# A two-block transformer layer on one core: how the chosen tokens are counted in the router, and which semaphores a few loads share

## The chip, the cores and the metric

The kernel runs on one core of a Trainium2 chip, written engine by engine: each engine has a program of its own, and they meet at semaphores. The metric is the device time of one execution in microseconds, the median of the runs. All data are float32.

## The reference, cut to what matters

Two blocks run one after the other on 256 tokens of width 1024. The first has a modulation, a Fourier and convolution mixer, and then an expert-choice layer of 16 experts. The second has two kinds of attention, a gate and a final norm. The change touches the router of the experts and some waits of the second block.

```python
logits = h @ w_router + b_router          # 256 tokens x 16 experts
probs = softmax(logits)
vals, idx = top_k(probs.T, 32)            # each expert takes 32 tokens
xe = h[idx]                               # 16 x 32 x 1024
y = (silu(xe @ w_gate_e) * (xe @ w_up_e)) @ w_down_e
x = x + gate_f * scatter_add(y * vals, idx)
x = rms_norm(x, g_final)                  # then the second block:
u = rms_norm(x, mix_norm_g) @ w_in_2      # q, k, v of both attentions, z
s = q @ k.T * scale + bias                # bias: slopes times distance, masks
```

The experts' weights are 16 x 3 x 8 MB, and each is read once.

## The kernel before

**Weights.** SyncE (SP) issues all large loads into a ring of 16 places of 1 MB in SBUF and a few more beside it (`ring`, `extra`, `late`). It waits until PE has released a place (`slot_used`), and then loads the next piece. `load_expert` (L601) loads the experts' pieces. For each expert PE computes the hidden products (`hidden_product`, L1142, 8 k-steps for gate and 8 for up, a place released after each), then the product with `w_down_e` (L1169), and scatters the rows into PSUM (L1180). The first expert's weights, and some of the second's, fit into the ring before routing is finished; after that SP has to wait for PE's first release.

**Router.** It runs once, between the mixer's last product and the first expert, on PE, DVE and ACT in turn. The order is: last quarters of `x` (L1994, L1995), turned by PE (`turn_x`, L1018) and kept (L2000); partial logits (`logit_parts`, L1026) copied by DVE (L2015); sums of the parts (L1068), `logit` (L2021), softmax, `prob` turned to expert rows (L1073). On those 16 rows of 256 tokens DVE takes the eight largest and strikes them out, four times (`V.max` L2033, `match_replace` L2034). Then it marks the struck ones (`is_lt`, L2036), sums the marks along the row with a scan (L2037) and multiplies sum and mark (L2038), which numbers each chosen token 1 to 32. PE turns these numbers back to token rows (L1082), DVE copies them (`slot_of`, L2040), builds the selection matrix of the first expert (L2042), PE gathers its rows (`gather`, L1090), DVE copies them, PE turns them (`turn_rows`, L1098), DVE scales and shifts them (L2052, L2054) into `cur[0]`, and the first hidden product starts.

**x's turns into banks.** The experts' results are added up in PSUM banks 4 to 7, which first get `x` itself, turned: 16 products of a 128x128 piece of `x` with the identity (L1077). In PE's program all 16 stand between the turn of `prob` and the turn of the numbers.

**Second block.** Its entry norm's gain `gfin` and the attention bias `bias` are loaded by GpSimd's queue (POOL). `gfin` (L714) is issued during the second expert. `bias` (3 MB, L716) goes to places of the ring that are free only late: POOL waits until PE has used the first weight piece of `q_diff`. They have a semaphore each, `side_loaded` and `bias_loaded`. DVE's program is in a fixed order; the part that matters is

```python
            split("k_diff", 0)
            dve.wait_ge(side_loaded, 16)
            # four products x * gfin into xg (L2252), each waits for a sum of squares
            split("k_diff", 1)
            norm_rows(2, halves=True)
            # further norms (roots by ACT, L1372), then
            split("q_dil", 0)
```

`split` turns a weight piece into a high and a low part: ACT copies the high part (L1380), DVE subtracts (L1763), and PE multiplies three times (L734 to L736, 24 such groups of one row or 5.5 us a piece here) only when the low part is there. `score_rows` (L2132) is the first that reads `bias`; its scores come from PE (L1222).

Of the kernel before, what the change touches and what calls it, by code (L numbers as in the profile page):

```python
# [20 lines left out]
ALU = mybir.AluOpType  # L21
# [3 lines left out]
P = 128  # L25
SEQ, D = 256, 1024
# [84 lines left out]
MIX_BANK = ((0, 2), (1, 3), (4, 5), (6, 7))  # L111
TURN_BANK = ((0, 0), (1, 1), (2, 2), (3, 0))

X_MIXED = 2 * WO


def build(nc, t, out):
    ctx = ExitStack()
    with ctx:
        def sem(name):  # L120
            return ctx.enter_context(nc.semaphore(name))
# [115 lines left out]
        logit_rows = gm_row[:, 256:512]  # L237
        left_t, order_t = gm_row[:, 256:512], squares_out[0]
        p_rows = shaped(gm_row[:, 512:1024], t=TT, c=SEQ)
# [33 lines left out]
        gain_loaded, gain_turned, gain_ready = sem("gain_loaded"), sem("gain_turned"), sem("gain_ready")  # L273
        dft_loaded, side_loaded, bias_loaded = (sem(n) for n in ("dft_loaded", "side_loaded", "bias_loaded"))
        late_loaded, row_bias_loaded = sem("router_and_gate_rows_loaded"), sem("row_bias_loaded")
# [32 lines left out]
        mask_ready, mask_turned = sem("mask_ready"), sem("mask_turned")  # L308
        gathered, rows_kept, rows_turned = sem("gathered"), sem("rows_kept"), sem("rows_turned")
        scaled, cur_ready, gw_turned, gwt_ready = sem("scaled"), sem("cur_ready"), sem("gw_turned"), sem("gwt_ready")  # L310
# [3 lines left out]
        p_loaded, pp_loaded, pp_done, pp_kept = sem("p_loaded"), sem("w_pp_loaded"), sem("pp_done"), sem("pp_kept")  # L314
        row_scale_ready, z_gated = sem("row_scale_ready"), sem("z_gated")
# [358 lines left out]
        def _(pool):  # L674
# [37 lines left out]
            pool.wait_ge(slot_used, HEAD_SLOTS + RING + 4)  # L712
            pool.dma_start(w_pp, rows_of(t["w_ple_proj_2"][0], (0, D), 0, 2)).then_inc(pp_loaded, 16)
            pool.dma_start(gfin, t["g_final"].partition_broadcast(P)).then_inc(side_loaded, 16)  # L714
            pool.wait_ge(slot_used, first_slot["q_diff"] + 1)
            pool.dma_start(bias, t["bias"].rearrange("(t p) h s -> p t h s", p=P)).then_inc(bias_loaded, 16)  # L716


        @block.tensor
        def _(pe):  # L720
# [337 lines left out]
            turn_x(3, (0,))  # L1058
            for i in range(3):
                pe.wait_ge(xt_act, i + 1)  # L1060
                logit_parts(i)
            pe.wait_ge(x_ready, 8)
            turn_x(3, (1,))
            pe.wait_ge(xt_dve, TT)
            logit_parts(3).then_inc(parts_done, 1)
            pe.wait_ge(parts_kept, 1)
            for tt in range(TT):
                last = mm(psum[:, 5, tt * NE:(tt + 1) * NE], logit_rows[:, tt * P:(tt + 1) * P], stack, start=True, stop=True)  # L1068
            last.then_inc(logits_done, 1)

# [31 lines left out]
            pe.wait_ge(slot_ready, 2)  # L1102
            gather(0)
            turn_rows(0, 1)

            def side_step(j):
# [7 lines left out]
                if j in (3, 5):  # L1114
                    n = j // 2 - 1
                    if n == 0:
                        pe.wait_ge(pt_ready, 1)
                        pe.wait_ge(pp_loaded, 16)
                    for tt in range(TT):
                        if n:  # L1120
                            pe.wait_ge(pp_kept, tt + 1)
                        for k in range(2):
                            last = mm(bank(tt), pt[k][:, tt * P:(tt + 1) * P], w_pp[:, k, n * BANK:(n + 1) * BANK], start=(k == 0), stop=(k == 1))
                        last.then_inc(pp_done, 1)

            def expert(i, h, looped=False, side=False):

                def weights(j, **dims):
# [5 lines left out]
                    return shaped(extra_slot(at) if at >= RING else ring[:, at, :], **dims)  # L1134

                def hidden_product(b):
# [9 lines left out]

                pe.wait_ge(cur_ready, 2 * i + (h + 1))
                hidden_product(0)
# [574 lines left out]
        def _(dve):  # L1723
# [294 lines left out]
            dve.wait_ge(logits_done, 1)  # L2018
            dve.wait_ge(base_ready, 1)
            for tt in range(TT):  # L2020
                ins = V.scalar_tensor_tensor(logit[:, tt, :], psum[:, 5, tt * NE:(tt + 1) * NE], stat[:, 1, 3, tt:tt + 1], base, ALU.mult, ALU.add)  # L2021
            link(ins)
# [8 lines left out]
            left = psum[0:NE, 1, 0:SEQ]  # L2031
            for _ in range(CAP // 8):
                link(V.max(top8[0:NE, :], left))  # L2033
                link(V.match_replace(left_t[0:NE, :], top8[0:NE, :], left, -1.0))  # L2034
# [20 lines left out]

            gathered_rows(0, 1)

# [188 lines left out]
            split("k_diff", 0)  # L2246
            dve.wait_ge(side_loaded, 16)
            for n in range(2):
# [139 lines left out]
```

## Time and profile before

| | |
|---|---|
| three runs | 1314.63, 1314.11, 1312.86 us; median 1314.11 |
| the profiled execution | 1314.88 us, its span 1313.1 us |
| PE busy | 979.5 us (75%) |
| DVE busy | 378.1 us (29%) |
| ACT busy | 247.5 us (19%) |
| DMA | 496.43 MB, mean 378 GB/s over the span |

The span runs from the first to the last instruction on the engines; 1.8 us of the execution lie around it. Times within the span are from its start. The mixer takes about 220 us, routing lies at 222 to 238 us, the experts reach to 1133 us, and the second block fills the rest. "PE", "PEld" (weight loads), "DVE", "ACT", "POOL" and "SPq" (SyncE's queue of DMA issues) are the engines of the rows. A row gives start, length, engine, line and operation, what it writes and reads, the count, and in brackets the idle time before it with what ended it.

### The profile page before, as it was taken

To read this page: it belongs to the slowest core of one execution; us is meant where nothing else is said; L and a number is where in the kernel's file an instruction comes from. 1 tells how busy PE (TensorE), PEld (TensorE's weight loads), DVE (VectorE), ACT (ScalarE), POOL (GpSimd) and SP (SyncE) were. 2 spreads that over 40 slices of the span, in tenths; PEclk is the share of its full clock that TensorE was granted. 3 is DMA by queue.
4 is the path that set the end of the run, shared out by engine and by line. 5 is a ranking of instruction groups with operands and counts; after the bars stand their busy time and mean duration, and the time that the engine had idled before them with its cause. 6 is when DMAs were issued, how large, how long until landed. Compare 5 with 4: busy or idle time off the path is not lost.

```text
span 1313.1 us, 15613 instructions
## 1 busy us (share of the span) xinstructions
PE 979.5 (75%) x6766; PEld 559.6 (43%) x6766; DVE 378.1 (29%) x575; ACT 247.5 (19%) x375; POOL 21.6 (2%) x47
## 2 busy tenths in 40 slices
PE   8999999878665665655656655657556666899998
PEld 7999998323121221212121221212121221478988
DVE  4698866210000110000010100000010100388865
ACT  4453434001000000000000000000000000467744
POOL 2000200000000000000000000000000000000000
PEclk8999999988787888689798878888786887999999
DMA  9998999899999999999999999999999999965230
GB/s 336 389 377 311 321 389 414 351 430 430 427 434 428 431 431 431 426 434 433 431 431 431 426 431 437 431 430 431 429 427 436 429 430 421 392 234 161 97 128 33
DMA packets 70156, 496.43 MB, mean 378 GB/s; under 512 B 4794, under 2 KB 26954, under 8 KB 49632
## 3 DMA queue, kind: packets, MB, share of 16 engines
q1 hardware_dynamic: 67792, 489.11, 90.4%
q0 software_dynamic: 2080, 6.55, 1.5%
q8 instruction: 35, 0.57, 0.2%
q10 hardware_dynamic: 240, 0.11, 0.0%
q14 instruction: 9, 0.07, 0.0%
HBM read 494.71 MB, written 1.06 MB: 378 GB/s over the span
## 4 chain that ended last, share of the span: by engine, by line
DMA 56%; PE 42%; DVE 1%; issue 1%; ACT 0%; ACTq 0%; SPq 0%; DVEq 0%
DMA ring<-in_w_down_e 23%; DMA ring<-in_w_up_e 18%; DMA ring<-in_w_gate_e 15%; PE psum L734 8%; PE psum L735 8%; PE psum L736 8%; PE psum L1142 7%; PE psum L1169 4%; PE psum L1180 1%; PE psum L885 1%; PE psum L1222 1%; PE psum L1077 0%; DMA arena<-in_b_ada 0%; PE psum L797 0%; PE psum L1257 0%
## 5 line engine op out<-in xcount | busy, mean ns | idle before, releaser
L1142 PE MATMUL psum<-ring,arena 128*32 128x512 f32 x2048 | 304.2, 743 | 192.8 <-DMA ring<-in_w_up_e 111.6
L1169 PE MATMUL psum<-ring,arena 128*32 128x512 f32 x976 | 162.2, 800 | 98.1 <-DMA ring<-in_w_down_e 97.5
L1142 PEld LDWEIGHTS psum<-ring,arena 128*32 128x32 f32 x2048 | 70.8, 130 | 385.8 <-issue 179.0
L1169 PEld LDWEIGHTS psum<-ring,arena 128*32 128x32 f32 x976 | 42.8, 137 | 203.9 <-issue 143.7
L1763 DVE TENSOR_TENSOR ring_r<-ring,ring_r 128x2048 fp32r<-128x2048 f32 x49 | 111.1, 2289 | 36.6 <-ACT ring_r L1380 36.4
L1540 ACT ACTIVATE arena<-psum 128x512 f32<-128x512 f32 x16 | 9.6, 598 | 535.2 <-PE psum L1142 535.2
L734 PE MATMUL psum<-ht_hi,ring_r 128*128 128x256 f32 x384 | 109.5, 285 | 0.0
L735 PE MATMUL psum<-ht_lo,ring_r 128*128 128x256 f32 x384 | 108.1, 281 | 0.0
L736 PE MATMUL psum<-ht_hi,ring_r 128*128 128x256 f32 x384 | 107.6, 280 | 0.0
L2081 DVE TENSOR_TENSOR arena<-psum,arena 128x512 f32<-128x512 f32 x32 | 20.6, 686 | 290.0 <-PE psum L1169 290.0
L1380 ACT ACTIVATE ring_r<-ring 128x2048 fp32r<-128x2048 f32 x49 | 92.4, 1910 | 29.2 <-PE psum L736 24.1
L2074 DVE TENSOR_TENSOR arena<-psum,arena 128x512 f32<-128x512 f32 x16 | 11.1, 692 | 270.9 <-ACT arena L1540 270.9
L734 PE MATMUL psum<-ring_r,ht_hi 128*128 128x256 f32 (+1 forms) x256 | 87.0, 340 | 0.2 <-issue 0.2
L736 PE MATMUL psum<-ring_r,ht_lo 128*128 128x256 f32 (+1 forms) x256 | 86.9, 339 | 0.0
L735 PE MATMUL psum<-ring_r,ht_hi 128*128 128x256 f32 (+1 forms) x256 | 86.1, 336 | 0.0
L734 PEld LDWEIGHTS psum<-ht_hi,ring_r 128*128 128x128 f32 x384 | 72.1, 188 | 1.9 <-issue 1.5
L736 PEld LDWEIGHTS psum<-ht_hi,ring_r 128*128 128x128 f32 x384 | 72.5, 189 | 0.0
L735 PEld LDWEIGHTS psum<-ht_lo,ring_r 128*128 128x128 f32 x384 | 72.4, 189 | 0.2
L1180 PE MATMUL psum<-arena 128*128 128x256 f32 x256 | 61.4, 394 | 13.6 <-DVE arena L2081 13.6
L1544 ACT ACTIVATE arena<-psum 128x512 f32<-128x512 f32 x16 | 9.6, 597 | 297.5 <-PE psum L1157 297.5
L1180 PEld LDWEIGHTS psum<-arena 128*128 128x128 f32 x256 | 48.6, 195 | 36.4 <-DVE arena L2081 30.1
L734 PEld LDWEIGHTS psum<-ring_r,ht_hi 128*128 128x128 f32 x256 | 48.1, 188 | 6.4 <-issue 1.1
(291 smaller groups left out, 921.8 us busy)
## 6 DMA issues: line engine op xcount, KB each, us to landing
ring<-in_w_gate_e SPq DMA_DIRECT2D x23, 4096.0 KB, 33.4
ring<-in_w_up_e SPq DMA_DIRECT2D x22, 4096.0 KB, 33.0
ring<-in_w_down_e SPq DMA_DIRECT2D x21, 4096.0 KB, 33.8
ring<-in_w_up_e SPq DMA_DIRECT2D x16, 2048.0 KB, 36.5
ring<-in_w_in SPq DMA_DIRECT2D x31, 1024.0 KB, 9.7
ring<-in_w_gate_e SPq DMA_DIRECT2D x14, 2048.0 KB, 36.2
ring<-in_w_down_e SPq DMA_DIRECT2D x14, 2048.0 KB, 36.9
ring<-in_w_ada SPq DMA_DIRECT2D x16, 1024.0 KB, 10.3
```

The lines of the kernel that those rows point to most:

```text
L734: mm(to, left[0], right[0], start=start, stop=False)
L735: mm(to, left[0], right[1], start=False, stop=False)
L736: return mm(to, left[1], right[0], start=False, stop=stop)
L885: last = mm(psum[32 * g:32 * g + 32, 6, st % 2 * P:(st % 2 + 1) * P], c_rep[:, k, :], w[:, kk, g * P:(g + 1) * P], start=(k == 0), stop=(k ...
L1142: last = mm(psum[32 * g:32 * g + 32, b, :].rearrange("s (q c) -> s q c", c=4), cur[h][:, k, :], w[:, g // 2, :, g % 2 * 4:g % 2 * 4 + 4], ...
L1169: last = mm(psum[32 * q:32 * q + 32, 2 + n, :], act_t[:, f % 4, (f // 4) * CAP:(f // 4 + 1) * CAP], w[:, kk, n * BANK:(n + 1) * BANK], sta ...
L1180: last = mm(bank(4 + q, c=2, s=SEQ)[:, c, :], y[:, n, at:at + P], gwt.rearrange("p t m -> p (t m)"), start=False, stop=True, skip_group_ch ...
L1222: last = mm(bank(4 + 2 * m + c, j=2, s=SEQ)[:, j, :], q[r, 2 * m + j, (a % 2) * P:(a % 2 + 1) * P], k[r, 2 * m + j, :], start=True, stop=T ...
L1380: f(ring_r[part_place[s]][:], ring[:, place(s), :], ACT.Copy).then_inc(hi_ready, 1)
L1763: V.tensor_tensor(ring_r[place(s)][:], ring[:, place(s), :], ring_r[part_place[s]][:].bitcast(F32), ALU.subtract).then_inc(lo_ready, 1)
L2074: V.tensor_tensor(sig_a, bank(0), sig_a, ALU.mult).then_inc(gated, 1)
L2081: V.tensor_tensor(y[:, n, :], bank(2 + n), gf_row[:, n * BANK:(n + 1) * BANK], ALU.mult).then_inc(y_ready, 1)
```

## The change

- **Counting.** The scan over 256 tokens in expert layout, the marks and their product leave DVE's chain. The struck-out rows are turned at once; DVE marks them in token layout (128 x 32), and PE counts with three products: a triangle of ones `upto` (identity scanned once, earlier, on DVE) for the tokens of the same half, and all ones for the half before. DVE multiplies count and mark into `slot_of`.
- **Logits by token halves.** The copy of the partial logits, the sums and `logit` are cut in two halves of 128 tokens, with one bank each. The third partial logit moves behind the last turn of `x`.
- **First rows.** `cur[0]` is scaled and shifted in two halves; PE starts its first hidden product on the first (`first_cur`) and waits for the second at k = 4.
- **x's turns into banks** are spread: 1, 3, 9, 1, 1 and 1 of the 16 at six points of PE's router program.
- **Semaphores.** `pp_loaded` and `bias_loaded` are gone. `w_pp` now counts on `p_loaded` (behind a wait for `p`), `bias` on `side_loaded`; DVE's waits for `gfin` and for `bias` both ask for 32.

```diff
-        left_t, order_t = gm_row[:, 256:512], squares_out[0]
+        left_t, upto = gm_row[:, 256:512], squares_out[0][:, 0:P]
+        chosen = shaped(soft_flat[:, 64:96], t=TT, e=NE)
...
             pool.wait_ge(slot_used, HEAD_SLOTS + RING + 4)
-            pool.dma_start(w_pp, rows_of(t["w_ple_proj_2"][0], (0, D), 0, 2)).then_inc(pp_loaded, 16)
+            pool.wait_ge(p_loaded, 16)
+            pool.dma_start(w_pp, rows_of(t["w_ple_proj_2"][0], (0, D), 0, 2)).then_inc(p_loaded, 16)
             pool.dma_start(gfin, t["g_final"].partition_broadcast(P)).then_inc(side_loaded, 16)
             pool.wait_ge(slot_used, first_slot["q_diff"] + 1)
-            pool.dma_start(bias, t["bias"].rearrange("(t p) h s -> p t h s", p=P)).then_inc(bias_loaded, 16)
+            pool.dma_start(bias, t["bias"].rearrange("(t p) h s -> p t h s", p=P)).then_inc(side_loaded, 16)
...
-            for i in range(3):
+            def logit_part(i):
...
+            x_back = [(k, tt) for k in (4, 5, 6, 7, 2, 3, 0, 1) for tt in range(TT)]
+
+            def turn_back(which):
+
+                for k, tt in x_back[which]:
+                    mm(bank(4 + k // 2, c=2, t=TT, m=P)[:, k % 2, tt, :], x[:, tt, k * P:(k + 1) * P], ident,
+                       start=(k % 2 == 0 and tt == 0), stop=(k % 2 == 1 and tt == TT - 1))
+
+            logit_part(0)
+            logit_part(1)
             pe.wait_ge(x_ready, 8)
             turn_x(3, (1,))
+            logit_part(2)
             pe.wait_ge(xt_dve, TT)
             logit_parts(3).then_inc(parts_done, 1)
-            pe.wait_ge(parts_kept, 1)
+            turn_back(slice(0, 1))
             for tt in range(TT):
-                last = mm(psum[:, 5, tt * NE:(tt + 1) * NE], logit_rows[:, tt * P:(tt + 1) * P], stack, start=True, stop=True)
-            last.then_inc(logits_done, 1)
+                pe.wait_ge(parts_kept, tt + 1)
+                mm(psum[:, LOGIT_BANK[tt], 0:NE], logit_rows[:, tt * P:(tt + 1) * P], stack, start=True, stop=True).then_inc(logits_done, 1)
+            turn_back(slice(1, 4))
...
             last.then_inc(prob_turned, 1)
-            for k in range(KD):
-                for tt in range(TT):
-                    mm(bank(4 + k // 2, c=2, t=TT, m=P)[:, k % 2, tt, :], x[:, tt, k * P:(k + 1) * P], ident,
-                       start=(k % 2 == 0 and tt == 0), stop=(k % 2 == 1 and tt == TT - 1))
+            turn_back(slice(4, 13))
 
             pe.wait_ge(mask_ready, 1)
             for tt in range(TT):
-                last = nc.tensor.transpose(psum[:, 0, tt * NE:(tt + 1) * NE], order_t[0:NE, tt * P:(tt + 1) * P], ident[0:NE, 0:NE])
+                last = nc.tensor.transpose(psum[:, 0, tt * NE:(tt + 1) * NE], left_t[0:NE, tt * P:(tt + 1) * P], ident[0:NE, 0:NE])
             last.then_inc(mask_turned, 1)
+            turn_back(slice(13, 14))
+            pe.wait_ge(mask_ready, 2)
+            mm(psum[:, 0, 2 * NE:3 * NE], upto, chosen[:, 0, :], start=True, stop=True)
+            mm(psum[:, 0, 3 * NE:4 * NE], ones, chosen[:, 0, :], start=True, stop=False)
+            mm(psum[:, 0, 3 * NE:4 * NE], upto, chosen[:, 1, :], start=False, stop=True).then_inc(mask_turned, 1)
...
             gather(0)
+            turn_back(slice(14, 15))
             turn_rows(0, 1)
+            turn_back(slice(15, 16))
...
                 def hidden_product(b):
                     for k in range(KD):
+                        if first and b == 0 and k == 4:
+                            pe.wait_ge(cur_ready, 1)
...
             mix_quarter(3, 0)
+            dve.wait_ge(squared, 2 + 2 * (WO - 1) + 1)
+            link(V.tensor_tensor_scan(upto, ident, ident, 0.0, ALU.add, ALU.max))
             mix_quarter(3, 1)
...
-            V.tensor_copy(logit_rows, bank(4)[:, 0:SEQ]).then_inc(parts_kept, 1)
+            for tt in range(TT):
+                half = slice(tt * P, (tt + 1) * P)
+                V.tensor_copy(logit_rows[:, half], bank(4)[:, half]).then_inc(parts_kept, 1)
...
-            link(V.tensor_scalar(left_t[0:NE, :], left_t[0:NE, :], 0.0, None, ALU.is_lt))
-            link(V.tensor_tensor_scan(order_t[0:NE, :], left_t[0:NE, :], left_t[0:NE, :], 0.0, ALU.add, ALU.max))
-            V.tensor_tensor(order_t[0:NE, :], order_t[0:NE, :], left_t[0:NE, :], ALU.mult).then_inc(mask_ready, 1)
+            ins.then_inc(mask_ready, 1)
             dve.wait_ge(mask_turned, 1)
-            link(V.tensor_copy(slot_of, bank(0)[:, 0:32].rearrange("p (t e) -> p t e", t=TT)))
+            V.tensor_scalar(chosen, shaped(psum[:, 0, 0:2 * NE], t=TT, e=NE), 0.0, None, ALU.is_lt).then_inc(mask_ready, 1)
+            dve.wait_ge(mask_turned, 2)
+            dve.wait_ge(mask_ready, 2)
+            link(V.tensor_tensor(slot_of, shaped(psum[:, 0, 2 * NE:4 * NE], t=TT, e=NE), chosen, ALU.mult))
...
-            gathered_rows(0, 1)
+            dve.wait_ge(gathered, 1)
+            V.tensor_copy(cur_rows[0], bank(2)[:, 0:HALF]).then_inc(rows_kept, 1)
+            dve.wait_ge(rows_turned, 1)
+            for half in range(2):
+                ms, ks = slice(2 * half, 2 * half + 2), slice(4 * half, 4 * half + 4)
...
+                V.tensor_tensor(cur[0][:, ks, :], cur[0][:, ks, :], spread(quad_shift), ALU.add).then_inc(cur_ready if half else first_cur, 1)
...
-                dve.wait_ge(bias_loaded, 16)
+                dve.wait_ge(side_loaded, 32)
...
             split("k_diff", 0)
-            dve.wait_ge(side_loaded, 16)
+            dve.wait_ge(side_loaded, 32)
```

## Rows read from the trace of the kernel before

**Rows 1.** The chain that ended last, shares of the span by engine.
```profile
DMA 56%; PE 42%; DVE 1%; issue 1%; ACT 0%; ACTq 0%; SPq 0%; DVEq 0%
```

**Rows 2.** Window behind routing: busy us of each engine, PE's granted clock, DMA share, GB/s.
```profile
236.00:240.00 4.00, 2.91 (x26) 1.12 (x30) 1.84 (x7) 0.00 (x0) 0.00 (x0) 1.00 0.25 43
```

**Rows 3.** Timeline of SP's queue around routing.
```profile
238.72 1.82 SPq L601 DMA_DIRECT2D ring<-in_w_down_e  x2
243.01 5.19 SPq L601 DMA_DIRECT2D ring<-in_w_gate_e  x2
```

**Rows 4.** Timeline of routing, the steps that the change touches.
```profile
220.94 1.06 PE L1026 MATMUL psum<-arena 128*32 128x256 f32 x12
...
223.63 0.42 DVE L2015 COPY arena<-psum 128x256 f32<-128x256 f32 x1 [0.46 <-PE psum L1026]
...
224.11 0.62 PE L1068 MATMUL psum<-arena 128*128 128x16 f32 x4 [0.53 <-DVE arena L2015]
...
224.83 0.38 DVE L2021 SCALAR_TENSOR_TENSOR arena<-psum,arena 128x16 f32<-128x16 f32 x2 [0.70 <-DVE arena L1747]
...
227.00 6.40 PE L1077 MATMUL psum<-arena 128*128 128x128 f32 x32
...
230.66 0.40 DVE L2034 MATCH_REPLACE8 arena<-arena 16x256 f32<-16x256 f32 x1
...
232.12 0.41 DVE L2038 TENSOR_TENSOR arena<-arena 16x256 f32<-16x256 f32 x1
...
233.33 0.29 PE L1082 MATMUL psum<-arena 16*128 16x16 f32 x2
233.66 0.19 DVE L2040 COPY arena<-psum 128x32 f32<-128x32 f32 x1 [1.13 <-PE psum L1082]
...
234.45 1.11 PE L1090 MATMUL psum<-arena 128*32 128x256 f32 x16 [0.83 <-DVE arena L2042]
...
237.12 0.42 DVE L2054 TENSOR_TENSOR arena<-arena 128x256 f32<-128x256 f32 x1
...
237.59 4.93 PE L1142 MATMUL psum<-ring,arena 128*32 128x512 f32 x44 [0.97 <-DVE arena L2054]
```

**Rows 5.** Group by line: a DVE copy of 128x128 from PSUM, mean ns last.
```profile
L2214 DVE COPY arena<-psum 128x128 f32<-128x128 f32 x1 | 0.3, 285 | 0.0
```

**Rows 6.** Windows where PE's clock changes, columns as in rows 2.
```profile
225.50:226.00 0.50, 0.00 (x0) 0.00 (x0) 0.20 (x2) 0.31 (x2) 0.00 (x0) 0.75 1.00 418
...
232.50:233.00 0.50, 0.50 (x6) 0.50 (x5) 0.04 (x1) 0.00 (x0) 0.00 (x0) 0.93 1.07 442
```

**Rows 7.** An expert's products behind 4 us of waiting, timeline of PE.
```profile
279.99 5.34 PE L1142 MATMUL psum<-ring,arena 128*32 128x512 f32 x32 [4.25 <-DMA ring<-in_w_up_e]
```

**Rows 8.** POOL's issue of `bias`: its timeline row, and its line's time to landing.
```profile
1142.88 0.70 POOL L716 DMA_DIRECT2D ring<-in_bias  x1 [881.81 <-PE psum L736]
```
```profile
DMA to landing us min/median/max: 13.6/13.6/13.6
```

**Rows 9.** Timeline of DVE at the second block's entry.
```profile
1147.32 2.48 DVE L2252 TENSOR_TENSOR arena<-psum,arena 128x512 f32<-128x512 f32 x4
1150.09 2.29 DVE L1763 TENSOR_TENSOR ring_r<-ring,ring_r 128x2048 fp32r<-128x2048 f32 x1 [0.28 <-ACT ring_r L1380]
...
1155.83 2.29 DVE L1763 TENSOR_TENSOR ring_r<-ring,ring_r 128x2048 fp32r<-128x2048 f32 x1 [1.51 <-ACT ring_r L1380]
...
1175.09 0.74 DVE L2206 TENSOR_SCALAR ring<-psum,arena 128x512 f32<-128x512 f32 x1
```

**Rows 10.** Timeline of ACT there: its split of q_dil's first piece.
```profile
1153.83 1.90 ACT L1380 ACTIVATE ring_r<-ring 128x2048 fp32r<-128x2048 f32 x1
```

**Rows 11.** Timeline of PE: k_diff's second piece begins, the first scores.
```profile
1155.26 0.39 PE L734 MATMUL psum<-ring_r,ht_hi 128*128 128x512 f32 x1
...
1175.94 2.00 PE L1222 MATMUL psum<-ring 64*128 64x256 f32 x16 [0.97 <-issue]
```

**Rows 12.** Windows from 1176 to 1312 us, their sum and mean.
```profile
sum 136.00, PE 132.19 PEld 117.72 DVE 99.81 ACT 81.68 POOL 0.00; mean PE 3.89 PEld 3.46 DVE 2.94 ACT 2.40 POOL 0.00
```

More of the change, by code:

```diff
@@ L112 @@
 TURN_BANK = ((0, 0), (1, 1), (2, 2), (3, 0))
+LOGIT_BANK = (5, 3)
 X_MIXED = 2 * WO
@@ L273, in build @@
         gain_loaded, gain_turned, gain_ready = sem("gain_loaded"), sem("gain_turned"), sem("gain_ready")
-        dft_loaded, side_loaded, bias_loaded = (sem(n) for n in ("dft_loaded", "side_loaded", "bias_loaded"))
+        dft_loaded, side_loaded = sem("dft_loaded"), sem("final_gain_and_bias_loaded")
         late_loaded, row_bias_loaded = sem("router_and_gate_rows_loaded"), sem("row_bias_loaded")
@@ L309, in build @@
         gathered, rows_kept, rows_turned = sem("gathered"), sem("rows_kept"), sem("rows_turned")
+        first_cur = sem("first_rows_half_scaled")
         scaled, cur_ready, gw_turned, gwt_ready = sem("scaled"), sem("cur_ready"), sem("gw_turned"), sem("gwt_ready")
@@ L313, in build @@
         pt_turned, pt_ready = sem("pt_turned"), sem("pt_ready")
-        p_loaded, pp_loaded, pp_done, pp_kept = sem("p_loaded"), sem("w_pp_loaded"), sem("pp_done"), sem("pp_kept")
+        p_loaded, pp_done, pp_kept = sem("p_and_w_pp_loaded"), sem("pp_done"), sem("pp_kept")
         row_scale_ready, z_gated = sem("row_scale_ready"), sem("z_gated")
@@ L1117, in side_step @@
                         pe.wait_ge(pt_ready, 1)
-                        pe.wait_ge(pp_loaded, 16)
+                        pe.wait_ge(p_loaded, 32)
                     for tt in range(TT):
@@ L1134, in weights @@
                     return shaped(extra_slot(at) if at >= RING else ring[:, at, :], **dims)
+                first = i == 0 and h == 0 if not looped else False
                 def hidden_product(b):
                     for k in range(KD):
+                        if first and b == 0 and k == 4:
+                            pe.wait_ge(cur_ready, 1)
                         if b and k == 4:
@@ L1145, in hidden_product @@
                         last.then_inc(slot_used, 1)
-                pe.wait_ge(cur_ready, 2 * i + (h + 1))
+                if first:
+                    pe.wait_ge(first_cur, 1)
+                else:
+                    pe.wait_ge(cur_ready, 2 * i + (h + 1))
                 hidden_product(0)
@@ L2014, in _ @@
             dve.wait_ge(parts_done, 1)
-            V.tensor_copy(logit_rows, bank(4)[:, 0:SEQ]).then_inc(parts_kept, 1)
+            for tt in range(TT):
+                half = slice(tt * P, (tt + 1) * P)
+                V.tensor_copy(logit_rows[:, half], bank(4)[:, half]).then_inc(parts_kept, 1)
             root_rows(1)
-            dve.wait_ge(logits_done, 1)
             dve.wait_ge(base_ready, 1)
             for tt in range(TT):
-                ins = V.scalar_tensor_tensor(logit[:, tt, :], psum[:, 5, tt * NE:(tt + 1) * NE], stat[:, 1, 3, tt:tt + 1], base, ALU.mult, ALU.add)
+                dve.wait_ge(logits_done, tt + 1)
+                ins = V.scalar_tensor_tensor(logit[:, tt, :], psum[:, LOGIT_BANK[tt], 0:NE], stat[:, 1, 3, tt:tt + 1], base, ALU.mult, ALU.add)
             link(ins)
@@ L2031, in _ @@
             left = psum[0:NE, 1, 0:SEQ]
-            for _ in range(CAP // 8):
+            for n in range(CAP // 8):
                 link(V.max(top8[0:NE, :], left))
-                link(V.match_replace(left_t[0:NE, :], top8[0:NE, :], left, -1.0))
+                ins = V.match_replace(left_t[0:NE, :], top8[0:NE, :], left, -1.0)
                 left = left_t[0:NE, :]
-            link(V.tensor_scalar(left_t[0:NE, :], left_t[0:NE, :], 0.0, None, ALU.is_lt))
-            link(V.tensor_tensor_scan(order_t[0:NE, :], left_t[0:NE, :], left_t[0:NE, :], 0.0, ALU.add, ALU.max))
-            V.tensor_tensor(order_t[0:NE, :], order_t[0:NE, :], left_t[0:NE, :], ALU.mult).then_inc(mask_ready, 1)
+                if n < CAP // 8 - 1:
+                    link(ins)
+            ins.then_inc(mask_ready, 1)
             dve.wait_ge(mask_turned, 1)
-            link(V.tensor_copy(slot_of, bank(0)[:, 0:32].rearrange("p (t e) -> p t e", t=TT)))
+            V.tensor_scalar(chosen, shaped(psum[:, 0, 0:2 * NE], t=TT, e=NE), 0.0, None, ALU.is_lt).then_inc(mask_ready, 1)
+            dve.wait_ge(mask_turned, 2)
+            dve.wait_ge(mask_ready, 2)
+            link(V.tensor_tensor(slot_of, shaped(psum[:, 0, 2 * NE:4 * NE], t=TT, e=NE), chosen, ALU.mult))
             for tt in range(TT):
@@ L2054, in gathered_rows @@
                 V.tensor_tensor(cur[h], cur[h], spread(quad_shift), ALU.add).then_inc(cur_ready, 1)
-            gathered_rows(0, 1)
+            dve.wait_ge(gathered, 1)
[3 more added lines that the diff above has]
+                ms, ks = slice(2 * half, 2 * half + 2), slice(4 * half, 4 * half + 4)
+                spread = lambda at: at[:, ks].unsqueeze(2).broadcast_to([P, 4, CAP])
+                turned = bank(2)[:, HALF:].rearrange("p (j m s) -> p m j s", j=2, s=CAP)[:, ms]
+                by_pairs = lambda at: at.rearrange("p (m j) s -> p m j s", j=2)
+                ins = V.tensor_tensor(by_pairs(cur[0][:, ks, :]), turned, by_pairs(spread(quad_scale)), ALU.mult)
+                if half:
+                    ins.then_inc(scaled, 1)
+                    dve.wait_ge(scaled, 1)
+                else:
+                    link(ins)
+                V.tensor_tensor(cur[0][:, ks, :], cur[0][:, ks, :], spread(quad_shift), ALU.add).then_inc(cur_ready if half else first_cur, 1)
             def take(picked, weighed):
```

## Prediction

> **What bounds the kernel now.** I read the chain that ended last first, to see which engine a saved microsecond must come from. It lies 56% in DMA and 42% in PE [rows 1]: in the long middle, from the first expert to the last, the weights' stream sets the time, and in the mixer and the second block PE does. Then I asked for windows and the timeline around routing, because the change is mostly there, and for SP's queue beside them. At 236 to 240 us the stream moves 43 GB/s, against some 430 elsewhere in the middle: all places of the ring are full. SP issues the next load only at 238.72 us, when PE has used the first piece of the first expert [rows 2, 3]. So routing, from the last quarter of `x` to the first hidden product at 237.59 us [rows 4], is on the path: whatever comes off it lets the stream restart earlier, and since everything to 1133 us then waits for that stream, it comes off the end too. The hole is some 5 us wide, so a gain up to about that size passes on whole.
>
> Last I looked for what the small edits touch, and that is the second block's entry. There DVE, ACT and PE hand each other pieces, and from 1176 to 1312 us PE is busy 132.2 of 136 us [rows 12]: a delay given to PE at the entry has nothing behind it that could take it back.
>
> **Logits by halves.** Before, the copy starts at 223.63 (0.42 us), the sums take 0.62, and `logit` is ready at 224.83 + 0.38 = 225.21 [rows 4]: 1.58 us. A copy of half the width takes 0.285 [rows 5]. After it PE sums the first half (0.31, half of 0.62), then the second (its copy was ready meanwhile), and DVE has one `logit` of some 0.2 left: 0.285 + 0.62 + 0.2 and about 0.15 of handovers make 1.26. Saved: 0.3. The third partial logit moves behind `x`'s last turn: the three took 1.06 us and ended at 222.00 [rows 4], so the turn can start at most a third of that, 0.35, earlier; it also needs `x`, and I take 0.2. The scan that makes `upto` is new on DVE, between the two last quarters, where DVE waits for PE's product of a whole w_o piece; it costs nothing. Were that cover gone, 128 elements a row would cost at most what the scan of 256 and the work behind it do now.
>
> **Counting.** The last strike-out ends at 230.66 + 0.40 = 231.06. Mark, scan and product end at 232.12 + 0.41 = 232.53. PE could then turn the numbers, but it is still in the 16 turns of `x`, from 227.00 for 6.40 us, and starts at 233.33; `slot_of` is there at 233.66 + 0.19 = 233.85 [rows 4]. That is 2.79 us, 0.80 of it the queue on PE. After: two turns 0.29; mark 0.19 (the size of the copy); three products with 16 columns, six instructions where four took 0.62, so 0.9; product 0.19; handovers 0.3. Sum 1.87, saved 0.9. One turn of `x` (0.2 us at full clock, 6.40/16 = 0.4 at half) lies under the mark, and the nine before it need 9 x 0.4 = 3.6 us at most, while DVE's four rounds end 231.06 - 227.00 = 4.1 us after the first of the turns starts; so PE's queue should not be late again, with 0.5 to spare.
>
> **First rows.** Scale and shift took 2 x 0.42 us and a handover [rows 4]; PE now starts after 2 x 0.285 [rows 5]. Saved 0.3. The second half is ready 0.6 us later, under four k-steps. A k-step takes eight instructions, 8 x 4.93/44 = 0.9 us [rows 4]. The turns of `x` beside the gather lie under DVE's copy and scaling.
>
> Sum of routing at full clock: 0.3 + 0.2 + 0.9 + 0.3 = 1.7 us.
>
> **PE's clock.** The granted clock fell to half (1.2 GHz) at about 225.75, when PE had stood since 224.73, and came back only at 232.5, after PE had been busy with `x`'s turns from 227.00 on [rows 6, 4]. So before, the gather and the first hidden product ran at 2.4 GHz thanks to those 16 turns in one piece. Now nine of them are done in 1.9 us at full clock, DVE needs 4.1, and PE stands for about 2 us just ahead of the count. Two bounds: the clock holds, and nothing is lost; or it falls, and the count (+0.4), the gather (1.11, +0.9), the turns (+0.3) and the first k-step (+0.9) run at half speed: 2.5 us, and routing is 0.8 slower than before. The nearest row is the fall at 225.75, after a shorter pause; but the clock may come back on the way. I take 0.9. Routing gives **0.8 us**, between -0.8 and 1.7.
>
> **The shared semaphore.** DVE's wait ahead of `xg` (L2252) asked for `gfin`, there for 850 us. It now asks for 32 on `side_loaded`, so for `bias` too. POOL issues `bias` at 1142.88, tied to PE's use of q_diff's first piece, and it lands 13.6 us later, at 1156.5 [rows 8]. DVE starts L2252 at 1147.32 [rows 9]. It will stand for 9.2 us. Queued behind it on DVE: the split of k_diff's second piece, the norms, every later split. I follow two chains.
>
> PE: the four products take 2.48 and the split ends 2.3 later, at about 1161.2. PE wanted that piece at 1155.26 [rows 9, 11]: it stands 6.0 us. Behind such a pause it starts at half clock: 32 instructions took 5.34 us after 4.25 of waiting, against 32 x 0.112 = 3.6 when warm, so 1.7 lost [rows 7, 4]. PE is then about 7.7 late.
>
> DVE and ACT: only 0.28 us of DVE's idle time goes (before the split at 1150.09), since the norms and ACT's root follow in a row, and ACT's split of q_dil starts at 1153.83 right behind the root; DVE's next split, at 1155.83, waits for it [rows 9, 10]. So this chain is 8.9 late. From there DVE is nearly always busy up to 1175.09 + 0.74 = 1175.83, and PE's first scores start 0.11 us after that [rows 9, 11]: DVE is what PE waits for there, so the 8.9 replace the 7.7, they don't add. Everything behind follows, PE being full [rows 12]. Term: **+8.9 us**; lower bound 6.0, if DVE makes up on the way and only PE's own stop counts; upper bound about 10, if PE's cold stretch is longer and ends later than DVE's chain.
>
> Here a rule decides how the wait is read. The Trainium skill, page "DMA: Bandwidth & Descriptors", section "Why a DMA increments its semaphore by 16 and not by 1", says that of two DMAs sharing a semaphore only the full count tells that both have landed. By it a wait for 32 ends with the last part of `bias`; were 16 of `gfin` enough, this term would be nothing and the time 1313.3. By that rule the landing above is the right moment; no run shown so far has such a wait.
>
> `w_pp`'s wait for `p` costs nothing: `p` is loaded over 30 us earlier, when the mixer ends.
>
> **Sum.** +8.9 - 0.8 = +8.1. On the profiled execution's 1314.88 us that is 1323.0. The runs' median is 0.77 lower, 1314.11, so I predict **1322.2 us**.
>
> **The rivals.** (a) PE's own stop decides and DVE catches up: 6.0 - 0.8 = +5.2, 1319.3 us. For it: DVE waits 1.51 us for ACT at 1155.83. Against: that wait is ACT's split, which is late by the same amount. Chance 0.12. (b) The clock stays low from the count through the first hidden product, and PE's cold stretch at k_diff ends later than DVE's chain: 10 + 0.8 = +10.8, 1324.9. For it: the fall at 225.75. Chance 0.13. (c) The other side: `bias` is there before DVE asks, since the loads around it are small or its transfer is quicker. Then only routing counts: 1313.3, or 1312.4 at full clock. It decides if `bias` lands within 1147.32 - 1142.88 = 4.4 us of its issue; 3 MB in that time would be 700 GB/s, and the trace has 13.6 us. Chance 0.07, mostly for something at the entry that I read wrong. My forecast has 0.68; its own range is 1320.5 to 1323.9, with the clock as its main unknown.
>
> **How the numbers follow.** About 0.2% (2.6 us) is what a measurement of this kernel can tell from no change. The forecast, (a) and (b) are all slower by more: 0.93. Of (c) 0.05 lies within 0.2%, and 0.02 is left for faster by more, which needs a routing gain of over 2.6 us, half as much again as my sum. The range goes from just below (a) to (b): 1318.8 to 1325.0.
>
> **What would show it.** DVE's L2252 should have about 9 us of idle time before it, ended by the DMA of `bias`, and PE a stop of about 6 us ahead of k_diff's second piece, at half clock behind it. The first hidden product should start at 235.9 to 237.6 us and SP's first later load a k-step after. The second block should begin about 0.8 us earlier. I would be wrong if DVE's idle time is there but the scores are late by much less than 8.9, or if routing gained over 2.6 us.

## The result, and the profile after

The changed kernel takes 1322.76 us (median of 4 runs, 1321.9 to 1323.55), the kernel before 1313.54 us beside it. The ratio is 1.0068, 95% interval 1.0056 to 1.0080: 7.4 to 10.5 us slower. All executions reported here ran at a mean granted clock of 0.87 to 0.89 but one: of e9's twelve below, one took 1565 us at 0.55, for a reason that nothing here shows, and is left out of e9's ratio. The profiled execution has a span of 1321.8 us, 8.7 more than before. Line numbers below are those of the changed kernel: L2302 is the product with `gfin` (L2252 before), L1792 DVE's split (L1763), L720 the issue of `bias` (L716), L1251 the scores (L1222), L738 to L740 PE's three products, L1073 x's turns, L1168 the hidden product.

Routing first. The timeline of the changed kernel, with the steps of [rows 4]:

```profile
223.06 0.49 DVE L2048 COPY arena<-psum 128x128 f32<-128x128 f32 x2 [0.46 <-PE psum L1030]
...
223.40 0.62 PE L1086 MATMUL psum<-arena 128*128 128x16 f32 x4
...
223.95 0.38 DVE L2054 SCALAR_TENSOR_TENSOR arena<-psum,arena 128x16 f32<-128x16 f32 x2 [0.33 <-PE psum L1086]
...
225.95 2.17 PE L1073 MATMUL psum<-arena 128*128 128x128 f32 x18
...
229.57 0.40 DVE L2067 MATCH_REPLACE8 arena<-arena 16x256 f32<-16x256 f32 x1
230.02 0.29 PE L1097 MATMUL psum<-arena 16*128 16x16 f32 x2 [1.90 <-DVE arena L2067]
...
231.55 0.19 DVE L2076 TENSOR_TENSOR arena<-psum,arena 128x32 f32<-128x32 f32 x1 [1.00 <-PE psum L1103]
...
232.34 1.93 PE L1110 MATMUL psum<-arena 128*32 128x256 f32 x16 [0.83 <-DVE arena L2078]
...
235.56 0.29 DVE L2100 TENSOR_TENSOR arena<-psum,arena 128x128 f32<-128x128 f32 x1 [0.79 <-PE psum L1118]
...
236.23 6.24 PE L1168 MATMUL psum<-ring,arena 128*32 128x512 f32 x48 [0.28 <-DVE arena L2106]
```

From copy to `logit`: 223.06 to 224.33, 1.27 us. From the last strike-out (229.97) to `slot_of` (231.74): 1.77 us instead of 2.79, and PE starts at 230.02, with nothing queued ahead of it; it stood for 1.90 us just before that. But the gather takes 1.93 us instead of 1.11. The windows say why (PE's granted clock is the third number from the end):

```profile
231.00:231.50 0.50, 0.50 (x4) 0.40 (x4) 0.00 (x0) 0.00 (x0) 0.00 (x0) 0.73 1.06 442
...
238.00:238.50 0.50, 0.50 (x12) 0.19 (x8) 0.00 (x0) 0.00 (x0) 0.00 (x0) 0.94 0.00 0
```

The clock falls to half at 231.2, behind PE's pause of 1.90 us and 1.2 us of work after it, and is back at 238.0. The first hidden product starts at 236.23 us, 1.36 earlier than before, and takes twice the time for its first pieces. So SP's queue gets only part of it, against [rows 3]:

```profile
238.22 1.21 SPq L604 DMA_DIRECT2D ring<-in_w_down_e  x2
242.54 5.17 SPq L604 DMA_DIRECT2D ring<-in_w_gate_e  x2
```

"Late" loads are those that had to wait for PE's first release. The first goes out 0.50 us earlier, and the first of 4 MB, the third late one, 0.47 us earlier.

Now the second block's entry. The chain that ended last, asked for from 1130 us on (start, length, what), its first pieces:

```profile
260.58 880.80 issue
1141.40 13.43 DMA ring<-in_bias
1154.85 2.48 DVE arena L2302 x4
1157.33 2.21 DVE ring_r L1792
1159.58 0.79 PE psum L738
```

The last four lines show how the loss begins: the transfer of `bias`, DVE's product behind it, DVE's split, PE. The line above them is a trap. On reaching POOL's issue the view goes back along POOL's own queue and books 881 us as "issue", and the page of this run then puts 67% of the span down to "issue". POOL did not set the time: its timeline row says that PE released it.

```profile
1141.40 0.70 POOL L720 DMA_DIRECT2D ring<-in_bias  x1 [880.82 <-PE psum L740]
```

Read such a chain from the end backwards, and stop where it jumps to an engine with nothing to do. Nor does the view settle which engine carries the loss on. From the last line it follows PE to the scores, and books PE's pauses just ahead of them (0.53, 0.45 and 1.37 us) as "issue". Before, these pauses were 0.53 and 0.97 us: PE stands longer there now, so something other than PE came last. e6 below decides it.

The rows that answer to [rows 8 to 11]; in the windows PE's clock again:

```profile
1154.85 2.48 DVE L2302 TENSOR_TENSOR arena<-psum,arena 128x512 f32<-128x512 f32 x4 [8.93 <-DMA ring<-in_bias]
...
1162.97 2.29 DVE L1792 TENSOR_TENSOR ring_r<-ring,ring_r 128x2048 fp32r<-128x2048 f32 x1 [1.51 <-ACT ring_r L1409]
...
1182.20 0.74 DVE L2256 TENSOR_SCALAR ring<-psum,arena 128x512 f32<-128x512 f32 x1
```
```profile
1159.58 0.79 PE L738 MATMUL psum<-ring_r,ht_hi 128*128 128x512 f32 x1 [5.65 <-DVE ring_r L1792]
...
1183.05 3.33 PE L1251 MATMUL psum<-ring 64*128 64x256 f32 x16 [1.37 <-issue]
```
```profile
1156.00:1158.00 2.00, 0.00 (x0) 0.00 (x0) 2.00 (x4) 1.23 (x3) 0.00 (x0) 0.56 1.03 379
...
1184.00:1186.00 2.00, 2.00 (x12) 1.58 (x8) 1.21 (x2) 0.00 (x0) 0.00 (x0) 0.50 0.00 0
```

I count from the entry, the start of DVE's last product of the expert stage (1131.09 after, 1132.57 before: 1.48 earlier). DVE stands 8.93 us. The scores come 51.96 us after the entry instead of 43.37: +8.6. The end comes 190.7 us after it instead of 180.5: +10.2. The last 1.6 us are new: PE made small pauses ahead of the scores, the clock fell once more at 1183.6, half a microsecond into them, and they took 3.33 instead of 2.00 us. The sum, -1.5 + 8.6 + 1.6, is the 8.7 us of the spans. The scores start 0.11 us after DVE's L2256 ends, as in [rows 9, 11].

### The profile page after: what moved, and what is told of

It reads as the page before. It is cut to its first block, busy times and chain, and to the rows that moved or that the text cites. A ratio compares the mean times of both kernels' runs of the same rounds, so it can differ in the third digit from the quotient of the medians.

```text
span 1321.8 us, 15630 instructions
## 1 busy us (share of the span) xinstructions
PE 989.2 (75%) x6772; PEld 562.1 (43%) x6772; DVE 377.4 (29%) x577; ACT 247.3 (19%) x375; POOL 21.3 (2%) x47
## 4 chain that ended last, share of the span: by engine, by line
issue 67%; PE 27%; SPq 2%; DMA 2%; DVE 1%; ACT 0%; POOL 0%; DVEq 0%; POOLq 0%
PE psum L738 7%; PE psum L739 7%; PE psum L740 7%; SPq L564 1%; PE psum L1168 1%; DMA ring<-in_bias 1%; SPq L574 1%; PE psum L1251 1%; DMA ring<-in_w_in 1%; PE psum L1286 0%; PE psum L1305 0%; PE psum L1314 0%; PE psum L1198 0%; PE psum L1324 0%; PE psum L983 0%
## 5 line engine op out<-in xcount | busy, mean ns | idle before, releaser
L1168 PE MATMUL psum<-ring,arena 128*32 128x512 f32 x2048 | 303.9, 742 | 182.9 <-DMA ring<-in_w_up_e 108.4
L1168 PEld LDWEIGHTS psum<-ring,arena 128*32 128x32 f32 x2048 | 70.2, 129 | 376.1 <-issue 174.0
L1792 DVE TENSOR_TENSOR ring_r<-ring,ring_r 128x2048 fp32r<-128x2048 f32 x49 | 111.1, 2287 | 37.0 <-ACT ring_r L1409 36.8
L738 PE MATMUL psum<-ht_hi,ring_r 128*128 128x256 f32 x384 | 109.5, 285 | 0.0
L740 PE MATMUL psum<-ht_hi,ring_r 128*128 128x256 f32 x384 | 107.6, 280 | 0.0
L738 PE MATMUL psum<-ring_r,ht_hi 128*128 128x256 f32 (+1 forms) x256 | 88.2, 345 | 5.9 <-DVE ring_r L1792 5.7
L740 PE MATMUL psum<-ring_r,ht_lo 128*128 128x256 f32 (+1 forms) x256 | 87.3, 341 | 0.0
L1209 PE MATMUL psum<-arena 128*128 128x256 f32 x256 | 63.7, 405 | 13.6 <-DVE arena L2131 13.6
L738 PEld LDWEIGHTS psum<-ht_hi,ring_r 128*128 128x128 f32 x384 | 72.2, 188 | 1.9 <-issue 1.5
L740 PEld LDWEIGHTS psum<-ht_hi,ring_r 128*128 128x128 f32 x384 | 72.5, 189 | 0.0
L738 PEld LDWEIGHTS psum<-ring_r,ht_hi 128*128 128x128 f32 x256 | 48.6, 190 | 12.8 <-DVE ring_r L1792 6.1
```

Source lines behind the costliest of these rows:

```text
L738: mm(to, left[0], right[0], start=start, stop=False)
L740: return mm(to, left[1], right[0], start=False, stop=stop)
L1168: last = mm(psum[32 * g:32 * g + 32, b, :].rearrange("s (q c) -> s q c", c=4), cur[h][:, k, :], w[:, g // 2, :, g % 2 * 4:g % 2 * 4 + 4], ...
L1209: last = mm(bank(4 + q, c=2, s=SEQ)[:, c, :], y[:, n, at:at + P], gwt.rearrange("p t m -> p (t m)"), start=False, stop=True, skip_group_ch ...
L1792: V.tensor_tensor(ring_r[place(s)][:], ring[:, place(s), :], ring_r[part_place[s]][:].bitcast(F32), ALU.subtract).then_inc(lo_ready, 1)
```

## The experiments

The kernel before, run beside the first eight of them, had a median of 1313.95 us; beside the last, 1314.28.

**e1: `bias` on its own semaphore again.**

```diff
-            pool.dma_start(bias, ...).then_inc(side_loaded, 16)
+            pool.dma_start(bias, ...).then_inc(bias_loaded, 16)
 # score_rows
-                dve.wait_ge(side_loaded, 32)
+                dve.wait_ge(bias_loaded, 16)
 # ahead of xg
-            dve.wait_ge(side_loaded, 32)
+            dve.wait_ge(side_loaded, 16)
```

> The changed kernel with a semaphore of its own for `bias` again, so that DVE's wait ahead of `xg` asks for `gfin` alone. Theory: the whole loss is that wait, and routing gave 0.5 to 1.5 us; the time is 1312.0 to 1313.2 us, DVE's L2252 has no idle time of a microsecond before it, and the first scores come about 45 us after the last scatter begins, as before. Rival (a loss elsewhere, in routing or in the order of x's turns): it stays above 1316.

Measured 1313.01 us, ratio 0.9990 (0.9981 to 0.9999). The timelines of DVE and SP:

```profile
1145.35 2.48 DVE L2302 TENSOR_TENSOR arena<-psum,arena 128x512 f32<-128x512 f32 x4
```
```profile
241.80 5.17 SPq L604 DMA_DIRECT2D ring<-in_w_gate_e  x2
```

There is no idle time before L2302, and from the entry (1130.60) to the scores it is 43.4 us again. The rest of the change, `w_pp`'s shared semaphore included, is worth 0.1 to 2.5 us.

**e2: the kernel before, with the shared semaphore alone.**

```diff
-            pool.dma_start(bias, ...).then_inc(bias_loaded, 16)
+            pool.dma_start(bias, ...).then_inc(side_loaded, 16)
-                dve.wait_ge(bias_loaded, 16)
+                dve.wait_ge(side_loaded, 32)
-            dve.wait_ge(side_loaded, 16)
+            dve.wait_ge(side_loaded, 32)
```

> The kernel before with nothing changed but the semaphore: `bias` counts on `side_loaded`, both of DVE's waits ask for 32. Theory: +9 to +10 us, 1322.8 to 1323.8, with 9 us of idle time before L2252. Rival (the wait costs only in combination with the new routing, or the new router costs several microseconds itself): clearly under +8.

Measured 1323.89 us, 9.9 more, ratio 1.0075 (1.0060 to 1.0091). DVE's timeline, and a window late in the second block:

```profile
1156.62 2.48 DVE L2252 TENSOR_TENSOR arena<-psum,arena 128x512 f32<-128x512 f32 x4 [8.91 <-DMA ring<-in_bias]
```
```profile
1269.60:1273.60 4.00, 3.85 (x14) 3.46 (x15) 3.97 (x8) 1.13 (x3) 0.00 (x0) 0.57 0.01 4
```

Three lines changed (one increment and two waits), and the whole loss is there. The scores come 52.1 us after the entry (1132.87), +8.7; here they run at full clock. The clock falls later, at 1270, behind a pause of 0.66 us behind which before's profiled execution kept it; end against entry is +10.3.

This run also gives a second profile of the old router, and shows how much of [rows 4] belongs to that one execution. Here the clock was low only from 225.5 to 228.9, fell again at 235.7, and PE was through with `x`'s turns in time:

```profile
226.36 4.93 PE L1077 MATMUL psum<-arena 128*128 128x128 f32 x32
...
231.94 0.29 PE L1082 MATMUL psum<-arena 16*128 16x16 f32 x2 [0.66 <-DVE arena L2038]
...
236.20 8.48 PE L1142 MATMUL psum<-ring,arena 128*32 128x512 f32 x64 [0.98 <-DVE arena L2054]
```

From the last strike-out to `slot_of` the old router takes 2.04 us here, not 2.79, and its first hidden product starts as early as the new one's. The start of that product is therefore no measure of the change. The third late load, at 243.04, is as late as before.

**e3: DVE splits k_diff's second piece before it waits.**

```diff
             split("k_diff", 0)
+            split("k_diff", 1)
             dve.wait_ge(side_loaded, 32)
...
-            split("k_diff", 1)
             norm_rows(2, halves=True)
```

> The changed kernel, shared semaphore kept, but DVE splits k_diff's second piece ahead of the wait, inside time that it would stand. If DVE's chain (norms, ACT's split of q_dil, the splits up to the turns) decides, it is shorter by one split, 2.2 us, and the time is 1320.3 to 1321. If PE's own stop at k_diff's second piece decides, that stop is gone, and the time falls by 6 us or more, to 1317 or less.

Measured 1321.09 us, ratio 1.0054 (1.0039 to 1.0070): 1.7 less than the changed kernel, with four executions of each. That is just above the range for DVE's chain and far from that for PE's stop. DVE and PE:

```profile
1155.28 2.48 DVE L2303 TENSOR_TENSOR arena<-psum,arena 128x512 f32<-128x512 f32 x4 [4.20 <-DMA ring<-in_bias]
...
1159.52 0.17 DVE L1776 RECIPROCAL arena<-arena 128x2 f32<-128x2 f32 x1 [1.48 <-ACT arena L1401]
```
```profile
1164.85 0.77 PE L738 MATMUL psum<-ring_r,ht_hi 128*128 128x512 f32 x1 [5.18 <-DVE ring_r L1792]
...
1182.55 2.00 PE L1251 MATMUL psum<-ring 64*128 64x256 f32 x16 [0.97 <-issue]
```

PE's stop at k_diff's second piece is gone, and one of 5.18 us stands at q_dil's first piece instead: PE waits for the same late chain, one piece further. The scores come 51.3 us after the entry (1131.29), 0.7 sooner than in the changed kernel, not the 2.2 of a whole split: DVE's reciprocal now stands 1.48 us for ACT's root, which has to wait until ACT has squared the two halves of the new `xg`. In the changed kernel DVE's split lay beside those squares and ended 0.5 us after them, so it was the last there, and ACT's root started 4.99 us after L2302. Without the split it starts 4.02 us after, and of that 1.0 us some 0.2 went to `bias`, which landed later against the entry. So the chain runs from the product with `gfin` over DVE's split, closely followed by ACT's squares, to the root. PE's own stop is not in it.

**e6: only a third of `bias` on the shared semaphore.**

```diff
+            pool.dma_start(bias[:, :, 0:4, :], by_head[:, :, 0:4, :]).then_inc(side_loaded, 16)
+            pool.dma_start(bias[:, :, 4:12, :], by_head[:, :, 4:12, :]).then_inc(bias_loaded, 16)
 # score_rows
                 dve.wait_ge(side_loaded, 32)
+                dve.wait_ge(bias_loaded, 16)
```

> The changed kernel, but only the first third of `bias` (1 MB) counts on the semaphore shared with `gfin`; the other two thirds have one of their own, asked for by the scores. Theory (DVE's chain decides, every microsecond that DVE stands ahead of `xg` comes out at the end): the third lands 5.5 to 7.5 us after its issue, DVE stands 1 to 3 us, and the time is longer than with the own semaphore by that much, 1314.2 to 1316. Rival (PE's stop at k_diff's second piece decides): PE had 2.9 us to spare there, so the time is that of the own semaphore, 1313.

Measured 1319.04 us, ratio 1.0040 (1.0025 to 1.0055), 6.0 more than e1 and far off my 1 to 3. The third landed 8.6 us after its issue, later than I had guessed.

```profile
1149.87 2.49 DVE L2305 TENSOR_TENSOR arena<-psum,arena 128x512 f32<-128x512 f32 x4 [4.10 <-DMA ring<-in_bias]
```
```profile
1154.61 0.50 PE L740 MATMUL psum<-ring_r,ht_hi 128*128 128x512 f32 x1 [0.82 <-DVE ring_r L1794]
...
1178.07 3.27 PE L1253 MATMUL psum<-ring 64*128 64x256 f32 x16 [1.37 <-issue]
```

DVE stands 4.10 us, PE only 0.82 at k_diff, PE's turns of the second block (L1286, here L1288) come 1.4 us late against the entry, and the scores come 47.1 us after it (1130.94): +3.8. So DVE's idle time comes out nearly one for one, as the theory has it, and PE's own stop does not count. The scores ran at half clock again (3.27 us), and end against entry is +5.2. My sum had missed the landing and this second fall of the clock, not the chain.

**e5: x's 16 turns in a row again, on top of e1.**

```diff
-            turn_back(slice(0, 1))
...
-            turn_back(slice(1, 4))
...
-            turn_back(slice(4, 13))
+            turn_back(slice(0, 16))
...
-            turn_back(slice(13, 14))
-            turn_back(slice(14, 15))
-            turn_back(slice(15, 16))
```

> The changed kernel with `bias` on its own semaphore, and x's 16 turns in a row behind the turn of `prob` again, everything else of the new router kept. Theory: the spread is worth 2 to 3 us by itself. With 16 turns in one piece PE is still in them when the struck-out rows are ready (at some 0.4 us a turn, if the clock falls ahead of them as it did in the kernel before), so the first hidden product starts 1.5 to 2.5 us later than in the run with the spread, at 238 to 239 us, and the time is 1313.5 to 1315. Rival: 16 turns at full clock take 3.5 us and are done in time, and they keep the clock up for the gather: then it starts at 235.3 to 236.3 us and the time is 1312 to 1313.

Measured 1315.31 us, ratio 1.0008 (0.9999 to 1.0017), 2.3 more than e1. PE's timeline and a window:

```profile
226.20 4.98 PE L1073 MATMUL psum<-arena 128*128 128x128 f32 x32
...
236.23 4.15 PE L1163 MATMUL psum<-ring,arena 128*32 128x512 f32 x24 [0.71 <-DVE arena L2101]
```
```profile
235.50:236.00 0.50, 0.02 (x1) 0.00 (x0) 0.41 (x2) 0.00 (x0) 0.00 (x0) 0.62 0.12 49
```

2.3 us is clear of the scatter of the executions, and the time lies just above the range of the theory. But both expectations were only half right. The clock was low for the first turns only, the row ended at 231.2, and the gather ran at full clock, so the hidden product started at 236.23, as early as with the spread (236.38 in e1). But then the clock fell at 235.6, the first pieces were slow, and the third late load went out at 243.02 instead of 241.80. The new counting, behind 16 turns that end at 231.2, takes 2.49 us from strike-out to `slot_of`, as PE's queue is late. Without the spread the new router gains nothing that could be measured; with it, the clock falls in another place.

**e4 and e7: dummy products where PE stands.** `keep_busy(n)` issues n products of ones with ones, 128x128, whose result nobody reads. e4 is e1 with one more line. e7 has it too, and needs no semaphore more than the changed kernel: `gfin` counts with `p` and `w_pp`, `bias` alone.

```diff
             turn_back(slice(4, 13))
+            keep_busy(7)
 # e7 besides
-            pool.dma_start(gfin, ...).then_inc(side_loaded, 16)
+            pool.dma_start(gfin, ...).then_inc(p_loaded, 16)
-                        pe.wait_ge(p_loaded, 32)
+                        pe.wait_ge(p_loaded, 48)
 # ahead of xg
-            dve.wait_ge(side_loaded, 32)
+            dve.wait_ge(p_loaded, 48)
 # score_rows
-                dve.wait_ge(side_loaded, 32)
+                dve.wait_ge(side_loaded, 16)
```

> As the run with a bias semaphore of its own, and with seven dummy products of 128x128 on PE behind the nine turns of `x`, where PE stood for 1.9 us in the changed kernel. Theory: the granted clock then stays full through the count and the gather (the gather took 1.93 us at half, 1.11 at full clock), and SP's first late load is issued 1.5 to 2 us earlier than with the gap; the time is 1.5 us below that run, 1310.5 to 1311.7. Rival: the clock falls anyway, or PE's queue is late for the turn of the struck-out rows; no gain.

> No semaphore more than in the changed kernel: `gfin` counts with `p` and `w_pp` (both waits ask for 48, met by 290 us), `bias` is alone on its own, and the seven dummy products stand behind the nine turns. Theory: the same as the filled run with a bias semaphore of its own, 1311.5 to 1312.4 us. Rival: PE's wait for 48 in the second expert costs, since `gfin` lands 28.5 us after its issue: then PE has idle time at L1112's successor at 285 to 307 us.

e4 took 1311.95 us, ratio 0.9988 (0.9979 to 0.9997), e7 1311.87 us, ratio 0.9981 (0.9972 to 0.9990). e4's timeline of PE:

```profile
232.23 1.11 PE L1111 MATMUL psum<-arena 128*32 128x256 f32 x16 [0.83 <-DVE arena L2079]
...
235.10 7.07 PE L1169 MATMUL psum<-ring,arena 128*32 128x512 f32 x64 [0.49 <-DVE arena L2107]
```

The gather takes 1.11 us again, and the third late load goes out at 240.52, 1.3 earlier than in e1. e4 is 1.1 us faster than e1 (11 executions each, standard error of the difference 0.4), less than the 1.5 expected; against before, the two intervals overlap. In e7's profiled execution the clock fell at 233.3, between gather and hidden product, and that load went out at 241.39, so seven dummies don't always hold it. e7's time is e4's, within its expected range: `gfin` on the semaphore of `p` costs nothing that could be measured.

**e8 and e9: more dummies**, on top of e7: six ahead of the second block's first scores (e8), or three between count and gather (e9).

```diff
 # e8
+                if name == "scale_row":
+                    for _ in range(6):
+                        mm(psum[:, 4, 0:P], ones, ones, start=True, stop=True)
 # e9
+            keep_busy(3)
             pe.wait_ge(slot_ready, 2)
             gather(0)
```

> As the run with `gfin` on the semaphore of `p`, and six dummy products on PE between the turns and the first scores of the second block, where PE is busy 2.5 of 4 us and where the clock fell in the profiled run of the changed kernel. Theory: the clock falls in some of the executions only, so the median gains 0 to 0.7 us: 1311 to 1312.2. Rival: the dummies delay the scores, which come as soon as DVE's last unit is ready: +0.3 to +0.6.

> As the run with `gfin` on the semaphore of `p`, with three more dummy products between the count and the gather, where PE stands for 0.8 us. In one of three profiled runs with seven dummies the clock held through the first hidden product, in two it fell at about 233.5 us. Theory: with the second filling it holds in all executions; SP issues its third late load at 240.5 us instead of 241.4, and the median falls by 0.5 to 1 us, to 1310.9 to 1311.4. Rival: what falls the clock lies before, or the dummies delay the gather: 1311.9 or more.

e8 took 1311.96 us, ratio 0.9984 (0.9975 to 0.9993), e9 1311.93 us with the same ratio and interval. In e9's profile the clock held through the first hidden product, and still the median did not move. In e8's the scores came 43.7 us after the entry instead of 43.4, the 0.3 that its rival named. e8 had little to win: in no profiled execution without a stall of DVE did the clock fall at the scores. Neither filling is worth anything that could be measured.

## Why the prediction was right, point by point

1322.2 us was predicted, 1322.76 measured, by the mechanism that was named. That the two are 0.6 us apart is in part luck: the change was forecast as +8.1 us and measured as +9.2, and the kernel before, measured beside it again, was 0.6 us below the 1314.11 that I had added to.

- **DVE's wait for `bias`**: 9.2 us forecast, 8.93 measured; `bias` landed 13.4 us after its issue (13.6 before). The three lines alone give the loss on the old router (e2) and their return removes it (e1). By the medians the shared semaphore costs 9.8 us (changed kernel against e1) to 9.9 (e2 against before); I had 8.9.
- **Which chain carries it**: DVE's and ACT's, +8.9 forecast at the scores, +8.6 and +8.7 measured. PE stopped 5.65 us (6.0 forecast) and was 7.5 late at the second block's turns (7.7), without adding. e6 shows it best: 4.1 us of idle DVE, 0.8 of idle PE, +3.8 at the scores. Rival (a), PE's own stop, fell there and in e3. The margin between the chains is small, though: in e2 PE's clock stayed low for some 6 us behind the stop instead of 3.5, the turns came 8.7 late, and DVE stood 0.17 us for them. Half of rival (b), a cold stretch that outlasts DVE's chain, came that near.
- **What the term left out**: I had PE full behind the scores and so no further loss. Later starts don't add one, but the clock does: in every profiled execution with a stall of DVE but e3's, it fell again somewhere behind, for 1.5 to 1.6 us. This is the term of the sum that was too small. The two profiled runs differ by +10.2 at the end, the edge of my upper bound.
- **Logits by halves**: 1.26 forecast for the stretch, 1.27 measured. **Third partial logit**: 0.2 forecast, and from `x`'s last quarter to the copy it is 2.64 us instead of 2.82. **Counting**: 1.87 forecast, 1.77 measured; but the saving of 0.9 was read against an execution in which PE's queue was 0.8 late for want of clock, and against e2's profile of the old router it is 0.3. **First rows**: 0.3 forecast; from the scaling to the first product 0.67 instead of 0.93. PE's queue was on time, as forecast.
- **PE's clock**: it fell behind the pause, as I feared, and stayed low through the gather and the first pieces. The forecast gain of routing was 0.8 us, and e1's median is 0.9 below that of before. The profiles show it best when `x`'s last quarter is taken as the start, since the mixer brings it at 220.2 us in one execution and at 221.1 in another. From there to the third late load it is 22.2 and 22.9 us with the old router (before, e2), 21.0 to 22.3 with the new one (changed kernel, e1, e3, e6), and 20.1 to 21.0 with dummies (e4, e7, e8, e9). In the changed kernel's profile it is 22.1: the steps saved 1.8 us and the clock took nearly all of it, where I had taken 0.9, a guess between two bounds. In e1's it took much less (21.2 us). I had also put it down to the 16 turns in one piece that the clock was full for before's first hidden product. e2 and e5 have such a piece too, and there the clock fell at 235.7 and 235.6, just ahead of that product.
- **From the load to the entry**: over the eleven profiled executions the entry comes 888.2 to 889.8 us after the third late load's issue. It follows the loads, as forecast, with a scatter of 1.6 us that is as large as the gain of this part. The entry is at 1130.6 to 1131.3 us in the four profiles of the new router without dummies and at 1132.6 and 1132.9 in the two of the old one.

By the medians, routing came out within 0.1 us of the forecast, well inside e1's interval of 2.4 us, so this proves little; and its parts did not hold so well: the gain of the counting depended on where the clock was low. The shared semaphore's term was 0.9 to 1.0 us too small, mostly for the clock's second fall.

## What to carry to other kernels

Before two loads share a semaphore, look at which of them lands last and who waits for the first: the early one inherits the landing of the late one, here 9 us for a semaphore saved, and in e7 pairing the early load with other early ones cost nothing that could be measured. Follow a stall through every engine that is handed something behind it, and take the longest chain, not the sum. Where small steps shorten a chain between engines, the gain can be lost to the clock of the engine that now stands: look at the granted clock there, try filling its pause, and look again. Here that was worth 1.1 us in e4 and nothing more in e8 and e9. And take a second profile of the kernel before: a step's gain read from one execution can be the clock's.

## What the runs showed of the hardware

The clock's fall is a matter of the execution, not only of the program. e1 and the changed kernel have the same router program, and the clock fell at 231.2 in the changed kernel and at 232.3 in e1, coming back at 238.0 and 235.7. Before and e2 share the old router, and its 16 turns took 6.40 us in one and 4.93 in the other. In the second block the same pauses ahead of the scores cost 1.3 us in the changed kernel and nothing in e3, nor in e2, where the clock fell behind another pause, 85 us later. A difference of 1.5 us between two profiled executions of such a kernel may be no more than that.

The transfer of a third of `bias` (1 MB) took 8.6 us to land, and the whole (3 MB) 13.4, each beside SP's loads of weights of 1 MB. So a third of the bytes still took almost two thirds of the time. In e6 the other two thirds were issued on the same queue only 0.7 us behind the first; how much of the 8.6 us they cost was not tested.
